# The last expert's gate matrix, transferred as parts of 119, 7 and 2 rows instead of one part of 128

## What is computed

```
def expert_block(args):
    xb, e = args
    hid = jax.nn.silu(xb @ w1[e]) * (xb @ w3[e])
    return hid @ w2[e]
...
out = jnp.zeros((n_tok + 1, dm), ys.dtype).at[slot_tok].add(ys)[:n_tok]
return rmsnorm(x, final_norm)
```

## Time and profile before

| what | value |
|---|---|
| median of the runs | 1469.81 us |
| the profiled execution's own time | 1470.11 us |
| its span, first to last instruction | 1468.4 us |
| mean granted TensorE clock | 0.985 |
| TensorE busy | 95% |
| read from HBM | 282.59 MB |
| time with the expert matrices streaming | from about 1040 us on |

### The profile page before, as it was taken

How to read it: one execution, slowest core, us unless ns; L and a number is a source line. 1 busy time by engine, 2 the same in 40 slices (tenths; PEclk the granted TensorE clock), 3 DMA queues, 4 the chain that set the end, 5 groups by cost and what they waited for, 6 DMA issues and landing times. The chain is left out here.

```text
span 1468.4 us, 27306 instructions
## 1 busy us (share of the span) xinstructions
PE 1391.6 (95%) x11354; PEld 1047.6 (71%) x11354; DVE 527.1 (36%) x1375; ACT 525.2 (36%) x1120; POOL 478.1 (33%) x457
## 2 busy tenths in 40 slices
PE   7999999989999999999989999999999999989976
PEld 6788876668788888888867787776666665556553
DVE  3102117750312200212143613355464454454435
ACT  4325447762422222222256532333322222222222
POOL 5334645524444444444455755320000000000000
PEclk9999999999999999999999999999999999999988
DMA  5223221104222223330332131659999999999994
GB/s 185 68 106 115 87 73 46 43 4 138 92 87 86 86 86 115 115 114 15 105 124 92 58 115 58 237 199 384 408 420 419 419 420 418 420 419 420 420 419 168
DMA packets 83900, 286.50 MB, mean 195 GB/s; under 512 B 8764, under 2 KB 31456, under 8 KB 59200
## 3 DMA queue, kind: packets, MB, share of 16 engines
q1 hardware_dynamic: 83376, 283.60, 49.6%
q0 software_dynamic: 288, 1.05, 0.2%
q10 hardware_dynamic: 112, 0.09, 0.0%
HBM read 282.59 MB, written 2.13 MB: 194 GB/s over the span
## 5 line engine op out<-in xcount | busy, mean ns | idle before, releaser
L485 POOL TENSOR_TENSOR wring_halves<-wring,wring_halves 128x512 fp32r<-128x512 f32 x274 | 357.6, 1309 | 381.8 <-ACT wring_halves L480 381.0
L480 ACT CAST wring_halves<-wring 128x512 fp32r<-128x512 f32 x274 | 168.5, 621 | 437.3 <-PE ps L1194 423.2
L1192 PE MATMUL ps<-wring_halves,big_halves 128*128 128x512 f32 x612 | 241.4, 394 | 3.8 <-POOL wring_halves L485 2.7
L1192 PE MATMUL ps<-hT_halves,wring_halves 128*128 128x512 f32 x480 | 187.4, 390 | 1.8 <-DVE big_halves L1925 1.8
L1194 PE MATMUL ps<-hT_halves,wring_halves 128*128 128x512 f32 x480 | 186.8, 389 | 0.0
L1193 PE MATMUL ps<-big_halves,wring_halves 128*128 128x512 f32 x480 | 186.8, 389 | 0.0
L2611 POOL TENSOR_TENSOR rstd<-rstd,half 128x1 f32<-128x1 f32 (+1 forms) x25 | 17.6, 709 | 518.4 <-DVE rstd L2564 480.2
L1193 PE MATMUL ps<-wring_halves,hT_halves 128*128 128x512 f32 x436 | 170.5, 391 | 0.0
L1194 PE MATMUL ps<-wring_halves,hT_halves 128*128 128x512 f32 x436 | 170.5, 391 | 0.0
L1192 PEld LDWEIGHTS ps<-wring_halves,big_halves 128*128 128x128 f32 x612 | 115.4, 189 | 31.8 <-POOL wring_halves L485 5.8
L1696 PE MATMUL ps<-xn,fixed 128*128 128x512 f32 x256 | 119.4, 608 | 1.1 <-DVE fixed L2359 1.1
(11 more groups left out here) (339 smaller groups left out, 2003.9 us busy)
## 6 DMA issues: line engine op xcount, KB each, us to landing
big<-in_moe_w_dram SPq DMA_DIRECT2D x90, 1024.0 KB, 25.5
wring<-in_moe_w_dram SPq DMA_DIRECT2D x70, 1024.0 KB, 25.4
wring<-in_ffn_w_in_dram SPq DMA_DIRECT2D x22, 1024.0 KB, 6.4
hT<-in_moe_w_dram SPq DMA_DIRECT2D x20, 1024.0 KB, 25.5
wring<-in_fox_w_in_dram SPq DMA_DIRECT2D x7, 2048.0 KB, 8.3
wring<-in_gla_w_in_dram SPq DMA_DIRECT2D x6, 2048.0 KB, 8.0
mkv<-in_moe_w_dram SPq DMA_DIRECT2D x12, 1024.0 KB, 26.1
wring<-in_ffn_w_out_dram SPq DMA_DIRECT2D x4, 2048.0 KB, 7.8
```

The source lines that it names most:

```text
L480: act.copy(hi, src).then_inc(s_hi, 1)
L485: pool.tensor_tensor(lo, src, hi, ALU.subtract).then_inc(s_lo, 1)
L1192: pe.matmul(out, lhs[1], rhs[0], start=start, stop=False)
```

## The change

The transfer of the gate matrix of the last expert (number 63, slot 3) is issued as three: rows 0 to 118, 119 to 125, and 126 and 127. Every other transfer stays whole. The loop over the extra blocks at the end passes a register as the number of the expert, so that it keeps whole transfers. The three parts add 48 to the semaphore where one added 16, so the wait of the last expert asks for 32 more.

```diff
+            LAST_PARTS = [(0, 119), (119, 126), (126, P)]
+
             def gate_up_in(e, j, last=None):
                 w13 = w13_slot(j)
                 if last is not None:
                     sp.wait_ge(s_gu, last)
                 for g, src in enumerate((W1, W3)):
-                    sp.dma_start(w13[:, g, :, :].rearrange("p k n -> p (k n)"), src[e]).then_inc(s_e13[j], 16)
+                    v = w13[:, g, :, :].rearrange("p k n -> p (k n)")
+                    parts = LAST_PARTS if isinstance(e, int) and e == EXPERTS - 1 and g == 0 else [(0, P)]
+                    for a, b in parts:
+                        sp.dma_start(v[a:b, :], src[e][a:b, :]).then_inc(s_e13[j], 16)
...
             def expert_in(b):
-                pe.wait_ge(s_e13[b % E_SLOTS], 32 * (b // E_SLOTS + 1))
+                pe.wait_ge(s_e13[b % E_SLOTS], 32 * (b // E_SLOTS + 1) + (32 if b == EXPERTS - 1 else 0))
```

## The result

The changed kernel takes 1479.4 us (median of 4 runs, 1477.54 to 1481.25) against 1469.51 us before, measured beside it (4 runs). The ratio is 1.0073, 95% interval 1.006 to 1.0085: 10 us slower, above the top of the predicted range. The profiled execution took 1480.72 us with a span of 1479.0.

A forecast was written before the change was run, and what follows sets the result against it. The prediction took HBM transfers to bound the expert stage, its end following the last matrix's landing. 1470.11 plus 1.3 for that landing gave 1471.4 us profiled, 1471.1 against the median; range 1466.6 to 1476.0.

The forecast's parts named there:

- What bounds the kernel, and that a later landing passes through whole: Expert stage: lasts as long as its bytes take; the kernel's end follows the last matrix's landing one to one.
- The clock of the tail: Last matmuls, half at 1.2 GHz: could move some 2 us either way; none in the sum, range widened by 0.5.
- Fewer rows for some engines, the term of -2.5 us: Last gate matrix: seven engines carry 18 or 19 rows, nine none; an engine without its eight rows ends 2.5 us earlier.
- wrong engines: Rival, chance 0.10: the seven engines that get more rows are among the late ones; 3.1 to 3.4 us, 1473.0.
- the prediction's own price: Seven carrying engines: 10 or 11 more rows at 0.313 us each, 3.1 to 3.4 us.
- The price of a row that goes elsewhere, the factor of 2 for the seven: Two engines writing the same partitions: 18 rows cost the seven 11.3 us, 8.8 more; last landing 1447.3, 1.3 later.
- the middle of 1438: Middle of 1436 to 1440, when the seven engines taken as early have done everything in the kernel before.
- Strong crowding: Rival, chance 0.20: SBUF side of the seven engines, factor 2.9 on 18 rows, 13.8 us more; 5.8 later, 1475.6.
- Issues on SyncE at nothing: Two more issues at the end cost up to 4.3 us, covered by the queue of waiting work, so nothing.
- The signs named for crowding: DMA share near 1 from 1430 to 1440, GB/s below 419, zero later than 1446, longer TensorE wait before expert 63.
- The chances: Whole kernel: below 1466.9 us 0.08, within 0.2% 0.58, above 1472.7 us 0.34.

The follow-up runs named there:

- The relief of the other eight: Kernel before, last gate matrix's upper 64 rows left out, lower 64 sent by eight transfers 4 partitions apart: 1469.89 against 1468.71 us, ratio 1.0005.
- 96 + 32: Transfers-only kernel, one matrix split into 96 and 32 rows between four whole ones and four: 2.1 and 2.7 us above the whole one's 24.8.
- 112 + 16: Last gate matrix as 112 and 16 rows: 1475.38 against 1469.71 us, ratio 1.0044; in the transfers-only stream 26.96 us against 24.95 whole.
- bare stream: Kernel without computation, one matrix split in some way between four whole transfers and four: whole 24.95 us, three pieces by columns 26.57, repeated 25.98 against 24.88.
- 124 + 4: Transfers-only kernel, one matrix split into 124 and 4 rows between four whole ones and four: 20.8 and 19.9 us above the whole one's 24.8.

## Why the prediction was wrong

Two steps failed, and the larger one is the price of a row that goes elsewhere.

*What bounds the kernel, and that a later landing passes through whole.* Nearly right: the landing for expert 63 moved by 12.0 us, the span by 10.6. But it was no longer the last down matrix that TensorE waited for; the chain behind the gate and up product, which ran at the lower clock, took over. The clock of the tail, left at nothing, gave back 2.4 us.

*Fewer rows for some engines, the term of -2.5 us.* The price of a row was right (3.2 us for ten), the number of engines too. The step that failed is that the seven who are done by 1436 to 1440 are the seven who carry the parts. That was only inferred from the number seven in both. By the landings of the changed kernel at least three of the carriers are among the nine late engines, and of eight engines that take 8 rows each two are, the last ones (2 us later for 2.5 us more work). The relief of the other eight gave nothing (-0.9 to +2.2 us by its interval). The rival "wrong engines" held this mechanism at 0.10. By the prediction's own price, 3.1 to 3.4 us would have been the result without any crowding; there was no gain to be had.

*The price of a row that goes elsewhere, the factor of 2 for the seven.* The mechanism was right, and the factor of 2 for a row as well: 205 GB/s at a share of 1.01 against 419. The mis-sized term is who pays it. The prediction charged it to the seven alone and let the nine stay at 1446, "as many rows still arrive in their partitions". In fact all 16 engines run at half speed for 11 us, and those still busy at some two thirds of it for 10 more; at least six of the nine landed at 1448.5 or later. At 228 GB/s the 22 us transfer what 12.0 us at 419 would. Of the 10 us that are missing, 0.08 x 22 = 1.8 are idle time of engines, the rest are slow rows. The count of rows in each partition is a lower bound for the time, and the prediction used it as the value. It also started the crowding at 1426 to 1430 for all seven. Its beginning in the windows is 1427, but it went on to about 1448, as it would be if the late ones among the seven get to the gate matrix some 10 us after the early ones. Why the rows of seven engines halve the mean rate of all 16 is shown by no run: with two engines to a place at most 14 would be slow. A slip of the working is small beside this: the middle of 1438 plus 8.8 is 1446.8, not 1447.3, so by its own terms the last landing was to be 0.8 us later and not 1.3.

*Strong crowding*, the rival at 0.20, was the right one in sign and place, with its price too small: 5.8 us, where the measurement says 10. It put 2.9 on 18 rows of early engines, which end at 1451.8 by it; with late engines among the seven the same working starts from 1446 and ends at 1459.8. The last landing was 1458.4.

*Issues on SyncE at nothing*: right. In the changed kernel the last issue ended earlier than before, and with three pieces by columns it ended 4.9 us later and made no difference. *The signs named for crowding* were right: share near one, bytes below 419, an end after 1446, a longer wait before expert 63. What they missed is the wait before expert 62.

*The chances.* 0.34 for slower by over 0.2%, and a top of 1476.0. The range ended at the strong crowding as priced. Added to the wrong engines, which no row excluded, it would have reached 1469.8 + 5.8 + 3.3 = 1478.9.

## What to carry to other kernels

Where a stream of transfers is the bound, keep each transfer over all 128 partitions. A split by rows that leaves the usual pairing of DMA engine and partitions slows everything in flight beside it, even if every engine has the same number of rows (96 + 32 cost 2.1 to 2.7 us for 1 MB, 112 + 16 cost 2.0 in a stream and 5.7 in this kernel). A split by columns cost nothing in the kernel (1.1 to 1.6 us in the bare stream). A DMA share near one with the GB/s at half is how it shows; and before shifting work from late to early engines, find out which engines these are, by adding work to some of them and reading when each share lands.

## What was not expected of the hardware

- Misplaced writes slow the transfers in flight beside them: 220 GB/s over 11 us at a share of 1.03, from 419, then 231 over 10 us, for 1 MB in 119, 7 and 2 rows.
- The 16 engines of one stream of whole transfers drift apart: after some 400 us the last matrix lands on the first engine at 1436.7 and on the last at 1446.4. What makes them drift stays open; the last matrix of a stream of nine lands on all 16 within 0.6 us.
- The same number of engines, transfers and source rows costs 0 or 4.6 us, only by the partitions that are written (4 apart or neighbouring).
- A single row decides the number of engines: 128 rows take 4.9 to 5.7 us alone, 127 rows 41.4, 126 rows 5.3 to 5.9, and 124 + 4 rows add 20 us to a stream, more than the 24 rows more on four engines (7.5 us) and what crowding cost the other splits. Why so much stays open.
